# The weight buffers 128 bytes off the activations' place in a line of 256, in place of 64

## What is computed

```python
u = h @ w_up
proj = jnp.einsum('bsd,de->bse', hn, w_in[l])
hg = jnp.einsum('td,edf->tef', h, w_gate[g])
```

## Time and profile before

| | |
|---|---|
| median of three runs | 992.86 us (990.83 to 993.28) |
| the profiled execution | 994.45 us, span 992.6 us |
| TensorE matmul busy | 949.6 us, 6339 instructions |
| VectorE, ScalarE busy | 463.8 us, 377.5 us |
| read from memory | 307.3 MB |
| mean granted clock of TensorE | 0.987 |

### The profile page before, as it was taken

How to read it: one execution, slowest core, us unless ns; L and a number is a source line. 1 busy time by engine, 2 the same in 40 slices (tenths; PEclk the granted TensorE clock), 3 DMA queues, 4 the chain that set the end, 5 groups by cost and what they waited for, 6 DMA issues and landing times.

```text
span 992.6 us, 15328 instructions
## 1 busy us (share of the span) xinstructions
PE 949.6 (96%) x6339; PEld 664.8 (67%) x6339; DVE 463.8 (47%) x859; ACT 377.5 (38%) x718; POOL 28.3 (3%) x60
## 2 busy tenths in 40 slices
PE   7899999998999999999988999999999999898987
PEld 5897777998999999988988444343434343332433
DVE  2787766676787477757875210212121212120113
ACT  2455555654665366544753312121212121110210
POOL 1000000000000000002130000000000000000000
PEclk9999999998999999999999899999999999999999
DMA  9967753734645543644658799999999999999996
GB/s 384 424 255 279 314 213 114 272 126 154 270 171 185 223 188 128 255 151 162 281 212 324 285 428 425 431 426 428 428 426 429 426 428 428 429 427 427 429 425 262
DMA packets 23398, 309.35 MB, mean 312 GB/s; under 512 B 2592, under 2 KB 3104, under 8 KB 4000
## 3 DMA queue, kind: packets, MB, share of 16 engines
q1 hardware_dynamic: 23184, 307.32, 76.1%
q10 hardware_dynamic: 144, 1.05, 0.3%
HBM read 307.31 MB, written 1.05 MB: 311 GB/s over the span
## 4 chain that ended last, share of the span: by engine, by line
PE 75%; DMA 13%; DVE 8%; ACT 2%; issue 1%; POOL 1%; DVEq 0%
PE ps L999 73%; DMA work<-experts 4%; DMA ring<-experts 4%; DMA slot<-experts 4%; DVE wl L1650 2%; DVE ring L1734 1%; PE ps L1209 1%; PE ps L1577 1%; DMA colT<-cols 1%; ACT wh L579 1%; POOL rstd L534 0%; PE ps L1519 0%; PE ps L1174 0%; ACT hH L805 0%; DVE xT L2086 0%
## 5 line engine op out<-in xcount | busy, mean ns | idle before, releaser
L999 PE MATMUL ps<-hH,wh 128*128 128x256 f32 x704 | 198.4, 282 | 3.6 <-DVE hL L1674 1.9
L1650 DVE TENSOR_TENSOR wl<-ring,wh 128x1024 fp32r<-128x1024 f32 (+1 forms) x136 | 163.7, 1214 | 71.7 <-ACT wh L579 71.4
L999 PE MATMUL ps<-hL,wh 128*128 128x256 f32 x704 | 195.9, 278 | 0.0
L999 PE MATMUL ps<-hH,wl 128*128 128x256 f32 x704 | 195.8, 278 | 0.0
L579 ACT ACTIVATE wh<-ring 128x1024 fp32r<-128x1024 f32 (+1 forms) x136 | 140.5, 1044 | 108.2 <-PE ps L999 86.0
L999 PEld LDWEIGHTS ps<-hH,wh 128*128 128x128 f32 x704 | 133.3, 189 | 6.1 <-issue 4.0
L999 PEld LDWEIGHTS ps<-hL,wh 128*128 128x128 f32 x704 | 133.4, 189 | 0.0
L999 PEld LDWEIGHTS ps<-hH,wl 128*128 128x128 f32 x704 | 133.3, 189 | 0.0
L2352 DVE SCALAR_TENSOR_TENSOR wc<-wc,w_slot,ps 128x512 f32<-128x512 f32 x16 | 12.0, 747 | 221.3 <-PE ps L999 221.3
L999 PE MATMUL ps<-aH,wh 128*128 128x256 f32 x304 | 84.8, 279 | 0.7 <-DVE wb L2207 0.7
L2345 DVE TENSOR_TENSOR eL<-ps,eH 128x512 fp32r<-128x512 f32 (+1 forms) x33 | 22.3, 675 | 133.9 <-ACT eH L982 73.7
(11 more groups left out here) (348 smaller groups left out, 1427.6 us busy)
## 6 DMA issues: line engine op xcount, KB each, us to landing
ring<-dense SPq DMA_DIRECT2D x39, 2048.0 KB, 8.4
ring<-experts SPq DMA_DIRECT2D x28, 2048.0 KB, 28.3
slot<-experts SPq DMA_DIRECT2D x28, 2048.0 KB, 29.3
work<-experts SPq DMA_DIRECT2D x20, 2048.0 KB, 28.7
early<-experts SPq DMA_DIRECT2D x10, 2048.0 KB, 27.0
wb<-experts SPq DMA_DIRECT2D x9, 2048.0 KB, 25.7
early<-dense SPq DMA_DIRECT2D x4, 2048.0 KB, 8.6
ring<-dense SPq DMA_DIRECT2D x4, 1024.0 KB, 5.8
```

What stands on the lines that cost most here:

```text
L999: return nc.tensor.matmul(o_, l, r, start=start, stop=stop, skip_group_check=True)
L1650: V.tensor_tensor(wl[:, c % CHUNKS, 0:n], src, wh[:, c % CHUNKS, 0:n].bitcast(F32), ALU.subtract)\
```

## The change

The first pad grows from 16 to 32 values of 4 bytes and the second shrinks from 48 to 32. The sum is the same. So `wl`, `wh`, `slot6` and `slot3` move by 64 bytes and lie 128 bytes after the place of the other large buffers; every other buffer stays where it was.

```diff
         early = sb("early", [P, UNIT])
 
-        sb("pad_weights", [P, 16])
+        sb("pad_weights", [P, 32])
         with nc.sbuf_tensor("wl", [P, CHUNKS, CHUNK], F32R) as wl:
             pass
         slot6 = sb("slot6", [P, SLOT])
         with nc.sbuf_tensor("wh", [P, CHUNKS, CHUNK], F32R) as wh:
             pass
         slot3 = sb("slot3", [P, SLOT])
-        sb("pad_stream", [P, 48])
+        sb("pad_stream", [P, 32])
         with nc.sbuf_tensor("hL", [P, KD, SEQ], F32R) as hL, nc.sbuf_tensor("hH", [P, KD, SEQ], F32R) as hH:
             pass
```

## The result

The changed kernel takes 1007.93 us (median, 1005.17 to 1010.22) against 992.27 us for the kernel before (990.83 to 993.28) in the same comparison. The ratio is 1.0155, with a 95% interval of 1.0122 to 1.0187. It is slower, by 15.7 us. The forecast of 993.0 us and its range up to 1007 us both missed.

The account below looks back on a forecast made before the run. TensorE's dense layers were taken to bound the kernel up to 545 us, the loads from 600 to 930 us. All terms summed to 0 us, so the forecast was the median, 993.0 us, with a range of 989 to 1007 us.

Parts of the forecast that it names:

- the first term: Dense matmuls with 256 streaming columns: fast and slow paces stay as now, 0 us; bounds -20 and +16.5 us.
- the ratio 6.0 to 4.5: Dense matmuls: ns over the fast pace at distance 0 and in 64's slow pace, read as meetings in a 256-byte line.
- Rival 1: Dense stretches stay at the slow 117.8 ns: 1000 us for one bad start, 1004.7 if none is fast; chance 0.20.
- Rival 2: Line of 128 bytes, so 128 equals distance 0: every dense matmul costs 119.3 ns, 1010 us; chance 0.14.
- Rival 3: Part of the fast pace's 6.6 ns over 106.7 is meeting and goes: 10.9 us less, 982 us; chance 0.16.
- with long streams the distance is worth 1 ns: Matmuls with 512 streaming columns: 229.3 against 230.0 ns; 348 with `wh`/`wl` streaming taken at 0, bounds -1 and +1 us.
- the small terms: Matmuls streaming `wh`/`wl` and the split: 0 each, bounds +-1 us; expert units in `slot3`/`slot6` and their loads: 0.
- The expert buffers and their loads: Expert stage, `slot3` and `slot6`: distance costs matmuls nothing (592 ns either way), target place shows nothing in loads (428 GB/s): 0.
- The gathers: Expert-stage matmuls where `pick` streams and aH/aL tokens are weights, at distance 0: keep 119.3 ns in all cases.
- The split: ScalarE's copy and VectorE's subtraction writing `wh` and `wl`, 1056 and 1229 ns per chunk: covered by TensorE, 0, bounds +-1 us.
- a microsecond of TensorE before 556 us is a microsecond of the end: Expert loads run back to back only once TensorE has used the first unit, so earlier TensorE time moves the end equally.
- The page's rule: TensorE's reads: by this rule every distance costs the same, change worth nothing; the prediction held 113.3 against 119.3 ns against it.

Follow-up runs that it names:

- bursts: Two test kernels of float32r matmul bursts at many distances (the second also other formats and weight-column counts), all of the kernel's other work left out: 474.34 and 437.53 us.
- off0: The whole kernel with the weight buffers at distance 0 in place of 64 from the streaming operands, against the kernel before: 1008.55 us beside 992.33.
- off192: The whole kernel with the weight buffers at distance 192 in place of 64, against the kernel before: 1001.59 us beside 992.33; repeated, 1002.21 against 994.74, ratio 1.0081.

## Why the prediction was wrong

- **The step that failed** is the first term: "At 128 they are as far from each other's start as they can be, so I take 113.3 ns for the matmuls that have it now". At 128, with 128 weight columns, the fast pace was never reached. Twelve of twelve repeated bursts and the dense part, but for two short stretches at 120.0, went at 118.7 ns. The term was not 0 but 2930 x 4.7 ns = 13.8 us, inside its own upper bound of 16.5 us and nearly all of the loss.
- **The reasoning beneath it** counted meetings by the ratio 6.0 to 4.5 and expected fewer with more distance. Cost doesn't fall with distance: 120.0 at 0, 113.3 at 64, 120.0 at 112, 118.7 at 128, 120.0 at 144, 117.8 at 192. Only one narrow place reaches 113.3 reliably. Three numbers, of which two were the two paces of one distance, could not carry a model of what lies between.
- **Rival 1** (the fast pace is not found) had the direction: "If no stretch reaches the fast pace it is 2600 x 4.5 = 11.7 us, 1004.7 us." No stretch did. But it held that the fast pace exists at 128 and is missed after some waits, and that the others go at 117.8; in no burst and no stretch at 128 was a fast pace seen at all, and the pace there is 118.7. That is 5.4 ns for each matmul that had been at 113.3 and 0.9 for each at 117.8. The range ended at 1007 us because it stood on 4.5.
- **Rival 2** (a line of 128 bytes) came near in size, 1010 us, and its sign is the one that the profile after shows: nearly one pace everywhere from the first chunk on (though 118.7 and not 119.3 ns), and means of 283 and more in the hH/hL groups. From that profile alone one could have taken it for true. The runs rule it out. It needed 0 and 128 alike, and 64 and 192 alike. The kernel at distance 0 packs 1336 matmuls into the window in which that at 128 has 1351, and the kernel at 192 loses 0.8% against that at 64. The argument against it in the prediction, that the ratio 6.0 to 4.5 spoke for 256 bytes, was right by result and weak by reason.
- **Rival 3** (faster than 113.3) found nothing: no distance, and no smaller weight load, went under it. That most of its excess over 106.7 "looks like the limit of the stream alone" fits: 113.3 is the lowest with 32 and with 64 weight columns too. What makes 256 float32r columns cost 113.3 and bfloat16 ones 109.2 wasn't tested.
- **A small misreading:** "with long streams the distance is worth 1 ns". In the bursts 512 streaming columns run from 228.8 to 233.3 ns between distances 0 and 64. The prediction compared two places that are both good for that shape: where the halves stream, the activations are what is loaded, so the distance counts the other way, and 64 is -64, or 192. It did no harm, as only some 200 matmuls follow each other in that form: 0.5 us.
- **Right:** the small terms. The expert buffers and their loads show no cost (ratio 0.9985). The gathers keep their pace, 119.4 ns on average after the change and 119.2 before. The split keeps its pace:

```profile
L1650 DVE TENSOR_TENSOR wl<-ring,wh 128x1024 fp32r<-128x1024 f32 x130 | 158.7, 1230 | 82.4 <-ACT wh L579 82.2
L579 ACT ACTIVATE wh<-ring 128x1024 fp32r<-128x1024 f32 x130 | 136.1, 1055 | 104.5 <-PE ps L999 96.2 <-DMA ring<-dense 8.0
```

  1230 and 1055 ns against 1229 and 1056, and ScalarE's wait for TensorE grew from 86.0 to 96.2 us, which is the loss seen from the producer's side. The claim that a microsecond of TensorE before 556 us is a microsecond of the end held: 10.2 us at the first gather, 10.8 in the span.
- **The page's rule** in the Trainium skill, "SBUF — State Buffer", section "Who interferes with whom" (two independent read ports, TensorE waits on nobody), would have given no change. The bursts agree for bfloat16 and float32 matmuls. For float32r at 256 columns they contradict it as far as it would make the place of the weights indifferent: 113.3 to 123.1 ns by distance, with none of the kernel's other work beside it.

What stays open is what picks a pace after a wait, whether 128 has a fast pace that is only very seldom found, why 192 finds the fast one in 3 of 12 repeated bursts and 64 in 12 of 12, and what in the reading makes 64 the good distance. The runs show that it is so, and no more.

## What to carry to other kernels

For back-to-back float32r matmuls with 128 weight columns and 256 streaming ones, put the loaded operand 64 bytes past the streaming one modulo 256, for every buffer of the sequence; here that is worth 15.7 us of 1008 against 128 bytes and about 16 against none (one run). It is no rule for other shapes: with 64 weight columns 64 bytes was the slowest of three distances, in one burst each. bfloat16 and float32 matmuls showed nothing of the kind. Read such an effect from distances between starts, or from the count in a full window, at two or more places in the trace: the pace can differ from one wait to the next. And where the trace holds no row for the new value, a mechanism with an extremum is not to be interpolated: the spread of the known values is then the size of the risk.

## What was not expected

- **More than one pace of one instruction at one place.** After each wait the sequence settles, at distances 64, 192 and 320, at 113.3 or at 117.8 ns and keeps it, in the kernel before for over 1550 matmuls. It does so in bursts with nothing of the kernel beside them too (the first burst of 48 at 64 was slow, the next four fast). Other distances have other pairs: 118.7 and 120.0 at 128, 113.3 and 120.0 at 52, 117.7 and 123.1 at 48.
- **The choice of distance turns with the shape.** 512 streaming columns want distance 0 or 192 (228.8 and 229.4 ns; 233.1 to 233.3 at 64 and 128), 256 columns want 64, 128 columns don't care (111.7). With 32 weight columns 128 bytes were as good as 64, with 64 weight columns 0 was the best of three, each in one burst.
- **The bursts forecast a second group of the kernel.** Where the halves stream over 512 columns, with the distance counted as loaded less streaming, the kernel's mean distances between starts are 228.1 ns at 0, 233.2 at 64, 232.6 at 128 and 230.3 at 192 (the versions off0, off192, after and before); the bursts gave 228.8, 233.3, 233.1 and 229.4.
- **One misplaced weight buffer costs nearly as much as two:** 117.9 ns on average with only `wh` at 128, against 118.7 with both and 114.0 with neither.
